# A hybrid attention and mLSTM layer on one core: the token transposes take over the scaling by the inverse roots

## The chip, the cores and the metric

The kernel runs on one core of one Trainium2 chip. The metric is the device time of one execution in microseconds (us), lower being better. The core has five engines that run side by side: TensorE (PE, with its weight loads shown apart as PEld), VectorE (DVE), ScalarE (ACT), GpSimd (POOL) and SyncE (SP), which issues most of the transfers. They synchronise through semaphores.

## The reference

The layer takes 1024 tokens of 1024 features. Only the first lines matter for this change:

```python
def rms_norm(x, w):
    xf = x.astype(jnp.float32)
    y = xf * lax.rsqrt(jnp.mean(xf * xf, axis=-1, keepdims=True) + RMS_EPS)
    return (y * w.astype(jnp.float32)).astype(x.dtype)

h = rms_norm(x, norm_w)
proj = jnp.einsum('btd,de->bte', h, w_in) + b_in
```

`proj` is 8720 columns wide. It is split into the inputs of a sliding-window attention and of an mLSTM. Their gated outputs go through two branch projections, a merge, an output projection with a residual, and a last RMS norm. Everything is fp32.

## The kernel before

**Tiling.** Tokens lie in `xs` as eight tiles of 128 tokens by 1024 features, tokens on partitions (`xs[:, t, :]`). The projection needs features on partitions, so TensorE turns every 128x128 block: `turn(t, k)` (L983 to L988) turns feature block `k` of token tile `t` into PSUM. Once the four tiles of a half (`t % 4 == 3`) are turned, block `k` of that half is a 128x512 tile in PSUM. ScalarE reads it, scales it by the norm weight and writes its high part in fp32r (`high_parts`, L1447, the operation at L1450); VectorE writes the low part, the rest (`low_parts`, L2121, the operation at L2125). The weights are split in the same way: `w_hi`, `w_lo`. A dense product is three fp32r products: high by high, low by high, high by low (`dense`, L957, the product at L973).

**The norm.** For tile `t`, ScalarE takes the sum of squares (`squares_of(t)`, L1441) once the tile has landed, VectorE makes a mean and adds epsilon (`variance(t)`, L2110), ScalarE takes the square root (`root(t)`, L1445), VectorE takes the reciprocal (L2114) and multiplies the whole 128x1024 tile in place (`normalised(t)`, L2119), and then TensorE may turn it (`turn_tile(t, ...)`, L993). Each queue is an order written out by hand.

**The order at the start.** TensorE: 24 transposes of the identity (L981), `turn_tile` 0 and 1, a transpose of the parameter rows (L1001) that ScalarE copies out (L1466), tile 2, the one block left out of tiles 0 to 2 (its bank held the parameters), tile 3, and then the first dense half tile (24 products, L1021), with `gate_tile(b, lo, hi)` (L1008, the product at L1015) beside the turns of the second half: four gate products, 12 turns of tiles 4 and 5, six gate products, 12 turns of tiles 6 and 7, six gate products, then the two blocks that found no free bank (8 turns), then the second dense half tile (L1035). From there on TensorE works through weight tiles that the other engines prepare: 32 pairs of tiles by a scheme of seven products (L1066), and the branch and output projections.

ScalarE: squares and roots of tiles 0 to 3 in turn (L1461), the copy of the parameters, `w_hi[0]` (L1469), `high_parts(0)`, squares and roots of tiles 4 to 7, `high_parts(1)`. VectorE: `variance` and `normalised` of tiles 0 to 3, `low_parts(0)`, the same of tiles 4 to 7, `low_parts(1)`. GpSimd waits for `w_hi[0]`, makes `w_lo[0]` in two halves (L828), and splits the gates' weights (L806, L808). SP issues the transfers: four tiles of x, the first weight tile, four more tiles of x (L582), the gates' weights as two transfers of 32-byte pieces (L584, L585), two gate biases, the sinks, and further weight tiles.

`ev` is an 8 KB buffer of two halves; the squares write their elementwise result, which nobody reads, to its first half.

Of the kernel before, what the change touches and what calls it, by code (L numbers as in the profile page):

```python
# [8 lines left out]
ALU = mybir.AluOpType  # L9
ACT = mybir.ActivationFunctionType  # L10
# [3 lines left out]
P = 128  # L14
# [3 lines left out]
NB = T // P  # L18
# [7 lines left out]
KB = 1024  # L26
# [94 lines left out]
def build(nc, x, norm_w, w_in, b_in, sinks, conv_w, conv_b, mnorm_w, wba, wbm, w_out, fnorm_w, out):  # L121
    ctx = ExitStack()
    with ctx:
        def sem(name):
            return ctx.enter_context(nc.semaphore(name))
# [5 lines left out]
        EV_AT = W_AT + 34 * KB  # L131
# [3 lines left out]
        def at(name, offset, shape, dt=F32):  # L135
            return nc.alloc_sbuf_tensor_at(name, shape, dt, offset=offset)

        def sb(name, shape, dt=F32):

            size = 4 if dt in (F32, F32R) else 2 if dt == BF16 else 1  # L140
            for n in shape[1:]:
                size *= n
            offset = kept[0]
            kept[0] += (size + 31) // 32 * 32
            return at(name, offset, shape, dt)
# [47 lines left out]
        w_raw = [at(f"w_raw{s}", W_AT + 4 * KB * s, [P, KT, P]) for s in range(2)]  # L193
        w_hi = [at(f"w_hi{s}", W_AT + o * KB, [P, KT, P], F32R) for s, o in enumerate((16, 8, 24))]
# [8 lines left out]
        squares = at("squares", W_AT + 20 * KB, [P, BANK])  # L203

        ev = at("ev", EV_AT, [P, 2, T])


        xs = at("xs", M_AT, [P, NB, T])
# [49 lines left out]
        ident = sb("ident", [P, P])  # L258
# [12 lines left out]
        rstd = sb("rstd", [P, 2 * NB])  # L271
# [18 lines left out]
        ps = ctx.enter_context(nc.psum_tensor("ps", [P, 8, BANK], F32))  # L290
# [32 lines left out]
        x_in = [sem(f"x_in{t}") for t in range(NB)]  # L323
        gate_slot_clear = sem("gate_slot_clear")
        w_in_sem = [sem(f"w_landed{s}") for s in range(2)]
# [3 lines left out]
        consts_made = sem("consts_made")  # L329
# [5 lines left out]
        x_norm = sem("x_norm")  # L335
# [106 lines left out]
        first_w_hi = sem("first_w_hi")  # L442
# [127 lines left out]
        x_rows = x.rearrange("(t p) d -> p t d", p=P)  # L570
# [5 lines left out]
        def _(sp):  # L576
# [1 line left out]
                sp.dma_start(xs[:, t, :], x_rows[:, t, :]).then_inc(x_in[t], 16)  # L578
            sp.dma_start(w_raw[0][:], w_cols[:, :, K0:K0 + P]).then_inc(w_in_sem[0], 16)

            for t in range(4, NB):
                sp.dma_start(xs[:, t, :], x_rows[:, t, :]).then_inc(x_in[t], 16)  # L582
            sp.wait_ge(gate_slot_clear, 1)
            sp.dma_start(w_raw[GATES][:, :, 0:8], w_cols[:, :, MI0:MF0]).then_inc(w_in_sem[GATES], 16)  # L584
            sp.dma_start(w_raw[GATES][:, :, 32:40], w_cols[:, :, MF0:MO0]).then_inc(w_in_sem[GATES], 16)  # L585
            sp.dma_start(gate_bias[0:8, :], b_in[MI0:MF0].rearrange("(h a) -> h a", a=1)).then_inc(vectors_in, 16)
            sp.dma_start(gate_bias[32:40, :], b_in[MF0:MO0].rearrange("(h a) -> h a", a=1)).then_inc(vectors_in, 16)
            sp.dma_start(sink_raw[:, :], sinks.partition_broadcast(P)).then_inc(vectors_in, 16)
# [107 lines left out]
            def weights(t0, tiles):  # L696

                cols = [c if isinstance(c, int) else sp.snap(c) for _, _, c in tiles]
                need = [n if isinstance(n, int) else sp.snap(n) for n in (t0 + j - 1 for j, _, _ in tiles)]
                for (j, src, _), c, n in zip(tiles, cols, need):  # L700
                    sp.wait_ge(w_split, n)
                    sp.sem_inc(passed, 1)

                    s = slot(BA + j)
                    sp.dma_start(w_raw[s][:], src[:, :, ds(c, P)]).then_inc(w_in_sem[s], 16)
# [248 lines left out]
        def _(pe):  # L954
# [27 lines left out]

            def turn(t, k):  # L983
                banks = BANKS[t // 4]
                mm = nc.tensor.transpose(ps[:, banks[k], (t % 4) * P:(t % 4 + 1) * P],
                                         xs[:, t, k * P:(k + 1) * P], ident[:])
                if t % 4 == 3:
                    mm.then_inc(x_turned, 1)  # L988

# [3 lines left out]
            def turn_tile(t, features):  # L993
                pe.wait_ge(x_norm, t + 1)
                for k in [k for k in range(features) if t >= 3 or k != table]:
                    turn(t, k)
# [7 lines left out]
            for t in range(3):  # L1004
                turn(t, table)
# [24 lines left out]
            for k in range(FRESH, KT):  # L1030
                pe.wait_ge(hT_lo_ready, KT + BANKS[1].index(BANKS[1][k]) + 1)
                for t in range(4, NB):
                    turn(t, k)
# [400 lines left out]
        def _(act):  # L1434
            A = nc.scalar.activation


            def squares_of(t):
                act.wait_ge(x_in[t], 16)
                act.drain()  # L1440
                A(ev[:, 0, :], xs[:, t, :], ACT.Square, accum_out=sumsq[:, t:t + 1]).then_inc(x_sumsq, 1)  # L1441

            def root(t):
                act.wait_ge(x_var, t + 1)
                A(rstd[:, t:t + 1], rstd[:, t:t + 1], ACT.Sqrt).then_inc(x_root, 1)  # L1445

            def high_parts(half):  # L1447
                for k in range(KT):
                    act.wait_ge(x_turned, KT * half + k + 1)
                    A(H[half][k // KH][0][:, k % KH, :], ps[:, BANKS[half][k], :], ACT.Copy,  # L1450
                      scale=par[:, R_NORM + k:R_NORM + k + 1]).then_inc(hT_hi_ready, 1)
# [3 lines left out]
            for row, src in ((R_NORM, norm_w), (R_Q, b_in[0:MI0]), (R_O, b_in[MO0:GM0 + D]), (R_MNORM, mnorm_w),  # L1455
# [2 lines left out]
                act.dma_start(param_rows[row:row + rows, :], src.rearrange("(r n) -> r n", n=P)).then_inc(params_in, 16)  # L1458
            act.dma_start(param_rows[R_CONVW:R_CONVW + 32, :],
                          conv_w.rearrange("j (r n) -> (j r) n", n=P)).then_inc(params_in, 16)  # L1460
            for t in range(3):  # L1461
                squares_of(t)
                root(t)
            squares_of(3)
            act.wait_ge(params_T, 1)
            A(par[:], ps[:, X[3], 0:ROWS], ACT.Copy).then_inc(params_ready, 1)  # L1466
            root(3)
            act.wait_ge(w_in_sem[0], 16)
            A(w_hi[0][:], w_raw[0][:], ACT.Copy).then_inc(first_w_hi, 1)  # L1469
            high_parts(0)  # L1470
            squares_of(4)
            squares_of(5)
# [631 lines left out]
        def _(dve):  # L2104
            V = nc.vector


            def variance(t):
                dve.wait_ge(x_sumsq, t + 1)
                V.tensor_scalar(rstd[:, t:t + 1], sumsq[:, t:t + 1], 1.0 / D, EPS, ALU.mult, ALU.add).then_inc(x_var, 1)  # L2110

            def inverse_root(t):
                dve.wait_ge(x_root, t + 1)
                return V.reciprocal(rstd[:, t:t + 1], rstd[:, t:t + 1])  # L2114

            def normalised(t):
                inverse_root(t)
                dve.drain()
                V.tensor_scalar(xs[:, t, :], xs[:, t, :], rstd[:, t:t + 1], None, ALU.mult).then_inc(x_norm, 1)  # L2119

            def low_parts(half):  # L2121
                for k in range(KT):
                    hi, lo = H[half][k // KH]
                    dve.wait_ge(hT_hi_ready, KT * half + k + 1)
                    V.scalar_tensor_tensor(lo[:, k % KH, :], ps[:, BANKS[half][k], :], par[:, R_NORM + k:R_NORM + k + 1],  # L2125
                                           hi[:, k % KH, :].bitcast(F32), ALU.mult, ALU.subtract).then_inc(hT_lo_ready, 1)

            for t in range(4):
                variance(t)
                normalised(t)  # L2130
            low_parts(0)
            variance(4)
            for t in range(4, NB):
                if t < NB - 1:
                    variance(t + 1)
                normalised(t)
# [664 lines left out]
```

## Time and profile before

| what | us |
|---|---|
| median of 3 runs (1077.52 to 1077.68) | 1077.52 |
| the profiled execution, its own time | 1077.55 |
| its span, first to last instruction | 1075.8 |
| TensorE busy | 1063.5 (99%) |
| VectorE busy | 725.9 (67%) |
| GpSimd busy | 649.7 (60%) |
| ScalarE busy | 516.9 (48%) |

The span is 1.75 us shorter than the time of the same execution. "Busy" counts an engine's instructions from start to end. TensorE's are pipelined, so what each costs in a stream is the distance between starts and not its duration. In a row of a timeline that covers several instructions of one kind, the second number runs from the first one's start to the last one's end; without the last one's own duration it is the distance from first to last start.

### The profile page before, as it was taken

The page shows a single profiled execution, that of the slowest core. Times are in us where ns is not written, and L with a number is a line of the kernel's source. Part 1 is how long each engine was busy: PE and PEld are TensorE (multiplying, and loading weights), DVE is VectorE, ACT ScalarE, POOL GpSimd, SP SyncE. Part 2 cuts the span into 40 slices and gives each one's busy share as a digit, 9 for nine tenths or more (in the row PEclk, how much of TensorE's full clock was granted, in tenths as well). Part 3 has the DMA queues.
Part 4 walks back from the last instruction along what each step waited for, and adds up shares of the span by engine and source line. Part 5 has one row for each costly group of instructions (what it writes and reads, how often), then busy time and mean ns, then how long its engine had stood idle before and what let it go on. Part 6 is the DMA issues. An engine that isn't in the chain of part 4 may idle for free.

```text
span 1075.8 us, 18631 instructions
## 1 busy us (share of the span) xinstructions
PE 1063.5 (99%) x6391; PEld 862.7 (80%) x6391; DVE 725.9 (67%) x1144; ACT 516.9 (48%) x1252; POOL 649.7 (60%) x437
## 2 busy tenths in 40 slices
PE   7999999999999999999999999999999999999997
PEld 6887887877877888878888888788788888888886
DVE  5964785776866967566756685669578332558897
ACT  7544755746647643555345444545464311132543
POOL 3577555556555568568955796679654354547441
PEclk9999999999999999999999999999999999999999
DMA  6235132132151231214211431143219434744324
GB/s 220 70 93 89 41 118 80 41 121 76 45 158 40 80 118 40 50 41 147 79 41 50 127 99 39 39 127 88 60 37 363 148 97 151 250 147 164 149 92 143
DMA packets 113851, 111.83 MB, mean 104 GB/s; under 512 B 7340, under 2 KB 96744, under 8 KB 112760
## 3 DMA queue, kind: packets, MB, share of 16 engines
q1 hardware_dynamic: 102648, 77.08, 24.2%
q10 hardware_dynamic: 11136, 33.88, 9.7%
q8 instruction: 39, 0.64, 0.2%
q14 instruction: 28, 0.23, 0.1%
HBM read 84.63 MB, written 26.31 MB: 103 GB/s over the span
## 4 chain that ended last, share of the span: by engine, by line
PE 97%; ACT 1%; DVE 1%; DMA 0%; DVEq 0%; issue 0%; ACTq 0%
PE ps L1066 64%; PE ps L1344 16%; PE ps L973 4%; PE ps L1178 3%; PE ps L1159 2%; PE ps L1233 2%; PE ps L1305 1%; PE ps L1287 1%; PE ps L1302 1%; ACT ev L1441 1%; PE ps L1299 1%; PE ps L1315 1%; PE ps L1253 1%; PE ps L1292 1%; PE ps L1015 1%; ACT h_hi L1450 0%
## 5 line engine op out<-in xcount | busy, mean ns | idle before, releaser
L823 POOL TENSOR_TENSOR ring_lo<-w,ring_hi 128x512 fp32r<-128x512 f32 x128 | 183.1, 1452 | 90.3 <-ACT ring_hi L1483 90.3
L823 POOL TENSOR_TENSOR ring_lo<-t,ring_hi 128x512 fp32r<-128x512 f32 x96 | 132.9, 1389 | 140.1 <-ACT ring_hi L1483 140.1
L1066 PE MATMUL ps<-s_hi,ring_hi 128*128 128x512 f32 x512 | 203.7, 398 | 0.0
L1066 PE MATMUL ps<-s_lo,ring_hi 128*128 128x512 f32 x512 | 200.2, 391 | 0.0
L1066 PE MATMUL ps<-s_hi,ring_lo 128*128 128x512 f32 x512 | 200.1, 391 | 0.0
L1066 PE MATMUL ps<-h_hi,ring_hi 128*128 128x512 f32 x384 | 151.6, 395 | 0.0
L1066 PE MATMUL ps<-h_lo,ring_hi 128*128 128x512 f32 x384 | 150.3, 392 | 0.0
L1066 PE MATMUL ps<-h_hi,ring_lo 128*128 128x512 f32 x384 | 149.9, 390 | 0.0
L1483 ACT ACTIVATE ring_hi<-w 128x512 fp32r<-128x512 f32 x128 | 77.0, 623 | 83.6 <-PE ps L1066 73.5
L1066 PEld LDWEIGHTS ps<-s_hi,ring_hi 128*128 128x128 f32 x512 | 96.2, 188 | 20.9 <-issue 2.5
L1066 PEld LDWEIGHTS ps<-s_hi,ring_lo 128*128 128x128 f32 x512 | 96.2, 188 | 20.0
L1066 PEld LDWEIGHTS ps<-s_lo,ring_hi 128*128 128x128 f32 x512 | 96.3, 188 | 18.4
L818 POOL TENSOR_TENSOR t<-w,t 128x512 f32<-128x512 f32 x64 | 96.8, 1512 | 9.0 <-issue 4.6
L1483 ACT ACTIVATE ring_hi<-t 128x512 fp32r<-128x512 f32 x96 | 59.9, 625 | 73.1 <-PE ps L1066 66.1
L806 POOL TENSOR_TENSOR w_hi<-w_raw,zero_col 128x1024 fp32r<-128x1024 f32 (+1 forms) x18 | 38.3, 2128 | 89.3 <-PE ps L1344 55.7
L1066 PEld LDWEIGHTS ps<-h_hi,ring_hi 128*128 128x128 f32 x384 | 72.3, 188 | 14.8 <-POOL ring_lo L823 0.7
L1066 PEld LDWEIGHTS ps<-h_hi,ring_lo 128*128 128x128 f32 x384 | 72.1, 188 | 14.8
L1066 PEld LDWEIGHTS ps<-h_lo,ring_hi 128*128 128x128 f32 x384 | 72.2, 188 | 13.9
L1344 PE MATMUL ps<-u_a,w_hi 128*128 128x512 f32 x256 | 78.9, 389 | 0.0
L1700 ACT ACTIVATE probs<-probs,neg_max 128x128 f32<-128x128 f32 x128 | 49.7, 390 | 41.3 <-DVE sink_in L2312 41.3
L1914 ACT ACTIVATE ev<-ev 128x1024 f32<-128x1024 f32 x16 | 17.0, 1062 | 107.6 <-DVE merged L2624 48.7
L1344 PE MATMUL ps<-u_m,w_hi 128*128 128x512 f32 x192 | 59.7, 392 | 0.0
(325 smaller groups left out, 2259.9 us busy)
## 6 DMA issues: line engine op xcount, KB each, us to landing
w<-in_w_in SPq DMA_DIRECT2D x128, 256.0 KB, 3.1
xs<-in_x SPq DMA_DIRECT2D x8, 512.0 KB, 7.5
ga_scratch<-ev ACTq DMA_DIRECT2D x4, 1024.0 KB, 4.2
u_scratch<-silu_z ACTq DMA_DIRECT2D x8, 512.0 KB, 3.2
c_rows<-c_scratch ACTq DMA_DIRECT2D x8, 512.0 KB, 6.1
gm_scratch<-ev ACTq DMA_DIRECT2D x4, 1024.0 KB, 5.0
w_raw<-in_w_branch_attn SPq DMA_DIRECT2D x8, 512.0 KB, 4.1
u_a_f<-u_scratch SPq DMA_DIRECT2D x4, 1024.0 KB, 8.4
```

The lines of the kernel that those rows point to most:

```text
L806: nc.gpsimd.tensor_tensor(hi, src, zero_col[:].to_broadcast(list(src.shape)), ALU.add)
L818: return nc.gpsimd.tensor_tensor(flat(dst), flat(a), flat(b), op)
L823: return nc.gpsimd.tensor_tensor(flat(lo[:]), flat(raw_or_sum[:]), flat(hi[:]).bitcast(F32), ALU.subtract)
L973: mm = nc.tensor.matmul(ps[:, 2 * s + b, :], w[:, k, :], h[:, k % KH, :], start=(r == 0), stop=(r == KT * TERMS - 1))
L1066: mm = nc.tensor.matmul(ps[:, bank, columns], w[:, k, :], h[:, k, columns], start=(m == 0), stop=(m == PRODUCT - 1))
L1159: mm = nc.tensor.matmul(ps[64 * half:64 * half + 64, SCORES[r], column:column + keys], q_T[rows, j, queries], k_now[rows, first:first + keys],
L1178: mm = nc.tensor.matmul(pv_ps(slice(64 * r, 64 * r + 64), half), v_m, pT[rows, 2 * r:2 * r + 2, queries], start=start, stop=stop)
L1233: mm = nc.tensor.transpose(ps[:, TURNED, h * P:(h + 1) * P], probs[n % 2][:, h, :], ident[:])
L1344: mm = nc.tensor.matmul(ps[:, 2 * s + b, :], w[:, k, :], part(k)[(0, 1, 0)[term]][:, token_half(b)], start=starts, stop=stops)
L1483: return A(ring_slot[0][:], raw_or_sum[:], ACT.Copy)
L1700: A(pr[:, h, :], pr[:, h, :], ACT.Exp, scale=HD ** -0.5, bias=neg_max[:, h:h + 1], accum_out=row_sum[:, h:h + 1])
L1914: A(ev[:, j, :], ev[:, j, :], ACT.Tanh, scale=0.5).then_inc(gate_tanh, 1)
```

## The change

The tokens are no longer multiplied in place. For each tile VectorE writes `scales[:, t, :]`, the 128x128 identity with row p times the inverse root of token p, into the second half of the `ev` buffer. `turn(t, k)` becomes an ordinary fp32 product of the raw block with `scales[:, t, :]`. On ScalarE the squares of tile t + 1 come ahead of the root of tile t for tiles 0 to 3, and `w_hi[0]` moves from ScalarE to VectorE, after the scaling of tile 3. On VectorE the variance of tile t + 1 comes ahead of the scaling of tile t, and VectorE waits for the identity. On SP the gates' weights are issued ahead of the last two tiles of x.

```diff
+        scales = at("scales", EV_AT + 4 * KB, [P, NB, P])
...
-            for t in range(4, NB):
+            for t in range(4, 6):
                 sp.dma_start(xs[:, t, :], x_rows[:, t, :]).then_inc(x_in[t], 16)
             sp.wait_ge(gate_slot_clear, 1)
             sp.dma_start(w_raw[GATES][:, :, 0:8], w_cols[:, :, MI0:MF0]).then_inc(w_in_sem[GATES], 16)
             sp.dma_start(w_raw[GATES][:, :, 32:40], w_cols[:, :, MF0:MO0]).then_inc(w_in_sem[GATES], 16)
+            for t in range(6, NB):
+                sp.dma_start(xs[:, t, :], x_rows[:, t, :]).then_inc(x_in[t], 16)
...
             def turn(t, k):
                 banks = BANKS[t // 4]
-                mm = nc.tensor.transpose(ps[:, banks[k], (t % 4) * P:(t % 4 + 1) * P],
-                                         xs[:, t, k * P:(k + 1) * P], ident[:])
+                mm = nc.tensor.matmul(ps[:, banks[k], (t % 4) * P:(t % 4 + 1) * P],
+                                      xs[:, t, k * P:(k + 1) * P], scales[:, t, :], start=True, stop=True)
...
-            for t in range(3):
+            squares_of(0)
+            for t in range(1, 4):
                 squares_of(t)
-                root(t)
-            squares_of(3)
+                root(t - 1)
             act.wait_ge(params_T, 1)
             A(par[:], ps[:, X[3], 0:ROWS], ACT.Copy).then_inc(params_ready, 1)
             root(3)
-            act.wait_ge(w_in_sem[0], 16)
-            A(w_hi[0][:], w_raw[0][:], ACT.Copy).then_inc(first_w_hi, 1)
             high_parts(0)
...
             def normalised(t):
                 inverse_root(t)
                 dve.drain()
-                V.tensor_scalar(xs[:, t, :], xs[:, t, :], rstd[:, t:t + 1], None, ALU.mult).then_inc(x_norm, 1)
+                V.tensor_scalar(scales[:, t, :], ident[:], rstd[:, t:t + 1], None, ALU.mult).then_inc(x_norm, 1)
...
+            dve.wait_ge(consts_made, 1)
+            variance(0)
             for t in range(4):
-                variance(t)
+                if t < 3:
+                    variance(t + 1)
                 normalised(t)
+            dve.wait_ge(w_in_sem[0], 16)
+            V.tensor_scalar(w_hi[0][:], w_raw[0][:], 1.0, None, ALU.mult).then_inc(first_w_hi, 1)
             low_parts(0)
```

## Rows read from the trace of the kernel before

**Rows 1.** The page: busy time of the engines over the span.
```profile
PE 1063.5 (99%) x6391; PEld 862.7 (80%) x6391; DVE 725.9 (67%) x1144; ACT 516.9 (48%) x1252; POOL 649.7 (60%) x437
```
**Rows 2.** The waits of TensorE, whole span: us in total, times, longest us.
```profile
PE ps L985 <- DVE xs L2119: 2.9, 5, 0.9
PE ps L981 <- POOL ident L795: 2.2, 1, 2.2
PE ps L973 <- DVE h_lo L2125: 0.9, 1, 0.9
```
**Rows 3.** The timeline, first half of the tokens: start us, us, instruction.
```profile
4.95 1.06 ACT L1441 ACTIVATE ev<-xs 128x1024 f32<-128x1024 f32 x1 [2.63 <-DMA xs<-in_x]
...
6.13 0.15 DVE L2110 TENSOR_SCALAR rstd<-sumsq 128x1 f32<-128x1 f32 x1 [6.13 <-ACT ev L1441]
...
6.79 0.75 DVE L2119 TENSOR_SCALAR xs<-xs,rstd 128x1024 f32<-128x1024 f32 x1
...
7.60 0.98 PE L985 MATMUL ps<-ident,xs 128*128 128x128 f32 x7 [0.92 <-DVE xs L2119]
...
11.39 1.04 ACT L1469 ACTIVATE w_hi<-w_raw 128x1024 fp32r<-128x1024 f32 x1
...
12.56 1.10 PE L985 MATMUL ps<-ident,xs 128*128 128x128 f32 x8 [0.34 <-DVE xs L2119]
12.93 4.74 ACT L1450 ACTIVATE h_hi<-ps,par 128x512 fp32r<-128x512 f32 x8 [0.50 <-PE ps L985]
...
14.55 0.47 PE L973 MATMUL ps<-h_hi,w_hi 128*128 128x512 f32 x1 [0.89 <-DVE h_lo L2125]
```
**Rows 4.** The same timeline, second half of the tokens.
```profile
18.98 1.06 ACT L1441 ACTIVATE ev<-xs 128x1024 f32<-128x1024 f32 x1
...
20.04 0.19 ACT L1445 ACTIVATE rstd<-rstd 128x1 f32<-128x1 f32 x1
...
20.50 0.75 DVE L2119 TENSOR_SCALAR xs<-xs,rstd 128x1024 f32<-128x1024 f32 x1
...
20.79 0.39 PE L1015 MATMUL ps<-h_lo,w_hi 128*128 128x512 f32 x1
...
21.31 0.88 PE L985 MATMUL ps<-ident,xs 128*128 128x128 f32 x6
...
24.74 1.47 PE L985 MATMUL ps<-ident,xs 128*128 128x128 f32 x12
...
28.54 0.50 PE L973 MATMUL ps<-s_hi,w_hi 128*128 128x512 f32 x1
```
**Rows 5.** The chain that ended last, a stretch of dense products: start us, us, what.
```profile
37.91 22.21 PE ps L973 x98
```
**Rows 6.** TensorE by line, an fp32 product: records, busy us, mean ns.
```profile
L1305 PE MATMUL ps<-v,dmat 128*128 128x129 f32 x128 | 20.0, 278 | 0.0
```
**Rows 7.** The timeline at 434 us: two fp32 products, their loads and their passes.
```profile
434.50 0.58 PEld L1305 LDWEIGHTS ps<-v,dmat 128*128 128x128 f32 x4
434.66 0.61 PE L1305 MATMUL ps<-v,dmat 128*128 128x129 f32 x4
```
**Rows 8.** Transfers of x: tiles 1 and 2 (L578), then the landings of tiles 4 to 7 (L582).
```profile
L578 SPq DMA_DIRECT2D xs<-in_x x2: 422/427/432, 1.3 to 1.7; - x2
DMA to landing us min/median/max: 4.9/5.4/5.9
...
DMA to landing us min/median/max: 8.2/8.7/10.0
```
**Rows 9.** The timeline of GpSimd, the low part of the first weight tile.
```profile
12.51 2.51 POOL L828 TENSOR_TENSOR w_lo<-w_raw,w_hi 128x512 fp32r<-128x512 f32 x2 [7.99 <-ACT w_hi L1469]
```
**Rows 10.** The timeline of SP's queue: the gates' second transfer, then a bias.
```profile
7.40 5.09 SPq L585 DMA_DIRECT2D w_raw<-in_w_in  x1
12.53 3.20 SPq L586 DMA_DIRECT2D gate_bias<-in_b_in  x1
```
**Rows 11.** All engines, 21 to 28.5 us; the last columns are PEclk, DMA share, GB/s.
```profile
21.00:28.50 7.50, 6.92 (x45) 5.62 (x44) 5.18 (x13) 4.80 (x12) 3.47 (x2) 1.00 0.23 67
```

## The prediction

> **What bounds the kernel now.** I read the page first: TensorE is busy for 99% of the span [rows 1]. Then its waits: it waits three times for another engine, 2.2 us for the identity, 2.9 us in five pieces for normalised tiles before a turn, 0.9 us for the first low part [rows 2], and all of it lies before 23 us. From there to the end no wait of TensorE is listed. So whatever delays the second dense half tile (28.54 us, [rows 4]) delays the end by as much, since every later stage starts from what TensorE has done. And the change can win at most what TensorE waits there. The question is how early the dense products start, and what TensorE itself must do before them.
>
> In the timeline a tile's chain is squares, mean, root, reciprocal, scaling, turn. The first tile's squares start at 4.95 when it lands, its turns at 7.60; the fourth tile's turns at 12.56, the first high part at 12.93, the first dense product at 14.55 [rows 3]. Between turns TensorE idles: seven take 0.98 us, and each next tile comes 1.65 us later.
>
> **What a turn costs.** This carries the forecast. Twelve transposes take 1.47 us from first start to last end [rows 4], one lasts 0.27, so starts lie (1.47 - 0.27) / 11 = 0.109 us apart; in short runs 0.118: (0.98 - 0.27) / 6 [rows 3]. The new turn is an fp32 product without the transpose flag. The kernel has such ones. The twelve transposes of tiles 6 and 7 have 12 records [rows 4]. L1305 is an fp32 product that the source issues twice for each of 8 chunks of 4 head pairs, 64 times, and it has 128 records [rows 6]: an fp32 product is two passes with two weight loads. Two of them together take 0.61 us for four passes, the last 0.275 long, so passes start (0.61 - 0.275) / 3 = 0.112 us apart [rows 7], with 129 columns. A new turn therefore holds TensorE for p = 2 x 0.112 = 0.224 us, against 0.11 to 0.12. Bounds: two passes at the transposes' pitch, 0.218; two at the pitch of the loads, (0.58 - 0.19) / 3 = 0.13 [rows 7], 0.26. I take 0.224, since shape, type and form are those of L1305.
>
> The trace knows a transposed block at 0.109 us and a pass of a product at 0.112, a ratio of 2.05 for the whole turn. The Trainium skill (TensorE: Matmul & The Clock Gate, Terms) says that the transpose mode makes fp32 four times faster; by that a turn would cost 4 x 0.109 = 0.436 us and the sum below would be 15.4 us. The trace does not agree for this shape.
>
> **Part 1, the first tiles.** Squares 1 can start when x tile 1 lands, 1.3 + 4.9 = 6.2 [rows 8], instead of 6.60. Its root of tile 0 now stands behind it: start 6.25 + 1.06 = 7.31 (a root follows squares by 1.06, 18.98 to 20.04 [rows 4]), end 7.50, scaling 0.27 later (20.23 to 20.50 [rows 4]) at 7.77. The scaling shrinks from 128x1024 to 128x128: 0.15 us is the length of a 128x1 operation, 0.75 that of the 1024-wide one [rows 3], so about 0.15 + 0.60 / 8 = 0.23. Turns of tile 0 start at 8.05, which is 0.45 later than now. Squares 2 and 3 follow at about 7.7 and 9.05; scaling 1 and 2 are ready at 9.5 and 10.9, and tile 3, with the parameters' copy between, at about 12.6.
>
> TensorE does not get there in time. Ahead of the first turn of tile 3 stand 7 + 7 + 7 + 3 = 24 turns and the transpose of the parameters (0.12): 8.05 + 24 x 0.224 + 0.12 = 13.55, against 12.56. From 8.05 on TensorE has no idle time, so earlier roots and shorter scalings buy nothing. The first high part needs one whole turn more, 0.11 longer than now. Delay of the first high part, and with it of the whole dense half tile: 13.55 - 12.56 + 0.11 = **1.10 us**. The other turns of tile 3 at 0.224 each stay ahead of the high parts, which go at 4.74 / 8 = 0.59 [rows 3].
>
> **Part 2, `w_hi[0]` on VectorE.** It leaves ScalarE, where it took 1.04 us ahead of the high parts in what was waiting time anyway [rows 3]: worth nothing. VectorE does it after scaling 3, from about 12.65, in 0.75 us by the row of the same shape [rows 3]; if its fp32r output halved the pace it would be 1.5. GpSimd then makes the first half of `w_lo[0]` in 1.25 us [rows 9], ready at 14.7 (or 15.4). The third dense product wants it at 14.55 + 1.10 + 0.45 = 16.1. Hidden, with 0.7 us left in the worse case. Were the cover gone, the cost would be that lateness. VectorE's low parts wait for the first high part, which starts at 14.03, so `w_hi[0]`, done at 13.4, does not hold them (at 14.15 it would not either, since the high part takes 0.59).
>
> **Part 3, tiles 4 to 7.** Take the times of before and add 1.10 at the end. The last of the first four gate products starts at 20.79; a 512-wide product holds TensorE 22.21 / 98 = 0.227 us [rows 5], so TensorE is free at 21.02, while the turns of tile 4 start at 21.31 [rows 4]. Scaling 4 now ends 0.53 earlier (20.73), and TensorE goes straight on: this gains 0.29, and the idle time before tile 5, some 0.5 us, is filled too. Then TensorE has 12 turns, 6 gate products, 12 turns, 6 gate products, 8 turns: 32 x 0.224 + 12 x 0.227 = 9.89, from 21.02 to 30.91. Squares go on at 1.33 us a tile, so scaling 5 (22.05) and 7 (24.3) are ready before their turns (22.4 and 26.4). The low parts that the last turns and the dense products wait for follow the first turn of tile 7 and are ready about 1.3 us before 30.9. Before, the first dense product of the second half streamed from 28.54 + 0.11 = 28.65 (it lasts 0.50 instead of 0.39, its load included). Delay: 30.91 - 28.65 = **2.26 us**.
>
> **Part 4, SP.** The two transfers of the gates' weights go past tiles 6 and 7. TensorE has no wait for their split even now [rows 2], and its first gate product comes 1.10 later: landing sooner gains nothing. Tiles 6 and 7 move behind an issue that took 5.09 us and another that took 3.20 [rows 10]; the cost of that is a rival. The wait for the identity on VectorE costs nothing, since TensorE has used it at 2.2 us [rows 2].
>
> **Sum.** 1.10 + 2.26 = +3.4 us; in general 57 p - 9.4. At 0.218 it is 3.0, at 0.26 it is 5.4. The profiled execution took 1077.55, within 0.03 of the median 1077.52. Forecast: 1080.9 us. The granted clock was 1.00 in this stretch [rows 11], so the prices are those of the full clock.
>
> **Rivals.**
> - *The new turn costs one pass* (the other side, not slower). Place: the 64 turns. Below p = 9.4 / 57 = 0.165 the change wins, and then other engines set the pace: tile 3 is scaled at about 11.6, its turns start 0.85 earlier, and in the second half some 0.5 of waiting goes. 1077.5 - 1.35 = 1076.2, which a measurement could hardly tell from no change. Against it: 128 records for 64 products. 4%.
> - *Only part of the delay gets through.* If the passes overlap better than rows 7 show, or the turns between gate products hide in their loads, p falls to 0.2 and the sum to 2.0: 1079.5. For it: short runs are read from few records. Against: TensorE shows no idle time among the short runs that such hiding could use. 9%.
> - *A turn costs four transposes.* Each of its two passes streams at half the pace of a transposed block, p = 4 x 0.109 = 0.436, and TensorE pays it 64 times: 57 x 0.436 - 9.4 = 15.4 us, 1092.9. Against: passes would start 0.218 apart and rows 7 have 0.112. 4%. (This is the skill's rule above.)
> - *Tile 7 lands late.* If SP is held for 5.09 us until 12.5 and for 3.2 more, and tile 7 needs the 10.0 us of the slowest x tile [rows 8], it lands at 25.7. Its squares, root and scaling take 2.1, and its turns are due at 27.5: 0.3 late, 1081.2; twice such holds would give 1084. For it: the small pieces really did hold the queue. Against: nearly 3 us of slack, and fewer bytes stand ahead. 8%.
> - *Forecast*: two passes at 0.218 to 0.26, 75%.
>
> **How the numbers follow.** About 0.2%, 2.15 us, is what a measurement of this kernel can tell from no change. The forecast case, the late tile and the four transposes are slower by more (87%, less a little for the forecast's lower edge: 86%). The middle case and the one pass lie within it (13%); I move 2 of these to a gain that I have not seen (the one pass with more waiting filled) and 1 from the slower cases: 3%, 11%, 86%. The range goes from 1079.2, which takes in most of the middle case, to 1083.0 (p = 0.26); outside are the one pass, the four transposes, and the edge of the late tile.
>
> **What would show it.** L985 should have 128 records instead of 64, with starts 0.11 us apart, and TensorE almost no wait between 8.05 and the dense products except for the first low part (0.9 or less). Turns of tile 0 near 8.05, first high part near 14.0, first dense product near 15.65, second dense half tile near 31.9. VectorE's scalings near 0.23 and `w_hi[0]` near 0.75. From there on both traces should run in parallel, 3.4 us apart. A first high part before 12.9, or 64 records, would make it wrong; so would a wait of TensorE after 32 us in the trace of before that I took for none.

## The result and the profile after

The changed kernel takes 1081.06 us (median of 7 runs, 1080.79 to 1081.37) against 1077.52 (1077.28 to 1077.68) beside it. The ratio is 1.0033, with a 95% interval of 1.0021 to 1.0045: it is 3.5 us slower. Its profiled execution took 1081.37, the slowest of the seven, with a span of 1079.7.

The page first, the line of engine busy times, against [rows 1]:

```profile
PE 1070.3 (99%) x6455; PEld 870.6 (81%) x6455; DVE 725.5 (67%) x1145; ACT 515.3 (48%) x1251; POOL 644.3 (60%) x437
```

TensorE has 64 records more and 6.8 us more busy time. The waits of TensorE over the whole span, against [rows 2] (us in total, times, longest):

```profile
PE ps L984 <- POOL ident L798: 2.2, 1, 2.2
PE ps L988 <- DVE scales L2120: 0.9, 1, 0.9
```

Of the five waits for a normalised tile one is left, the first; the wait for the first low part is gone too. Nearly all of that waiting has been filled, and the kernel is slower all the same. The operations by line within the first 34 us say with what (records, busy us, mean ns):

```profile
L988 PE MATMUL ps<-scales,xs 128*128 128x128 f32 x128 | 15.4, 277 | 0.9 <-DVE scales L2120 0.9
...
L2120 DVE TENSOR_SCALAR scales<-ident,rstd 128x128 f32<-128x128 f32 x8 | 2.3, 286 | 0.6
```

The 64 turns have 128 records, as the L1305 products had [rows 6]. The timeline, against [rows 3, 4] (start us, us, instruction):

```profile
6.06 1.06 ACT L1444 ACTIVATE ev<-xs 128x1024 f32<-128x1024 f32 x1
...
7.87 1.06 ACT L1444 ACTIVATE ev<-xs 128x1024 f32<-128x1024 f32 x1 [0.57 <-DMA xs<-in_x]
...
7.92 3.64 PE L988 MATMUL ps<-scales,xs 128*128 128x128 f32 x28 [0.92 <-DVE scales L2120]
...
9.39 0.29 DVE L2120 TENSOR_SCALAR scales<-ident,rstd 128x128 f32<-128x128 f32 x1
9.73 1.64 PEld L988 LDWEIGHTS ps<-scales,xs 128*128 128x128 f32 x14 [0.18 <-DVE scales L2120]
...
11.51 4.19 PE L988 MATMUL ps<-scales,xs 128*128 128x128 f32 x36
...
12.54 0.69 DVE L2136 TENSOR_SCALAR w_hi<-w_raw 128x1024 fp32r<-128x1024 f32 x1
13.31 2.50 POOL L831 TENSOR_TENSOR w_lo<-w_raw,w_hi 128x512 fp32r<-128x512 f32 x2 [8.81 <-DVE w_hi L2136]
...
14.17 4.74 ACT L1453 ACTIVATE h_hi<-ps,par 128x512 fp32r<-128x512 f32 x8 [2.10 <-PE ps L988]
...
15.78 0.47 PE L976 MATMUL ps<-h_hi,w_hi 128*128 128x512 f32 x1
...
22.27 2.84 PE L988 MATMUL ps<-scales,xs 128*128 128x128 f32 x24
...
26.34 2.84 PE L988 MATMUL ps<-scales,xs 128*128 128x128 f32 x24
...
32.10 0.48 PE L976 MATMUL ps<-s_hi,w_hi 128*128 128x512 f32 x1
```

The first dense product is 1.23 us later than before (15.78 against 14.55), the second dense half tile 3.56 later (32.10 against 28.54). A long run of 24 passes takes 2.84 us, the last 0.27 long: (2.84 - 0.27) / 23 = 0.112 us from start to start. After that both traces run in parallel. Two pieces of the chain that ended last, from the middle and from the start of the output projection (the kernel before has the same pieces at 798.20 and 993.37):

```profile
801.72 15.00 PE ps L1069 x66
...
997.25 70.78 PE ps L1069 x312
```

The distance is 3.52 us at 800 us and 3.88 at 997. The medians are 3.54 apart, so the last third of a microsecond probably belongs to this execution, the slowest of the seven. The profiled execution of one other kernel, turns_twice, shows the same step, from 17.09 to 17.43; what makes it stays open.

### The profile page after: what moved, and what is told of

It is laid out like the page before. It is cut to its first block, busy times and chain, and to the rows that moved or that the text cites. A ratio compares the mean times of both kernels' runs of the same rounds, so it can differ in the third digit from the quotient of the medians.

```text
span 1079.7 us, 18760 instructions
## 1 busy us (share of the span) xinstructions
PE 1070.3 (99%) x6455; PEld 870.6 (81%) x6455; DVE 725.5 (67%) x1145; ACT 515.3 (48%) x1251; POOL 644.3 (60%) x437
## 4 chain that ended last, share of the span: by engine, by line
PE 98%; DVE 1%; DMA 0%; ACT 0%; DVEq 0%; issue 0%; SPq 0%; ACTq 0%
PE ps L1069 63%; PE ps L1347 16%; PE ps L976 4%; PE ps L1181 3%; PE ps L1162 2%; PE ps L1236 2%; PE ps L1308 1%; PE ps L988 1%; PE ps L1290 1%; PE ps L1305 1%; PE ps L1302 1%; PE ps L1018 1%; PE ps L1318 1%; PE ps L1256 1%; PE ps L1295 1%; DMA xs<-in_x 0%
## 5 line engine op out<-in xcount | busy, mean ns | idle before, releaser
L826 POOL TENSOR_TENSOR ring_lo<-w,ring_hi 128x512 fp32r<-128x512 f32 x128 | 186.5, 1478 | 96.0 <-ACT ring_hi L1484 96.0
L809 POOL TENSOR_TENSOR w_hi<-w_raw,zero_col 128x1024 fp32r<-128x1024 f32 (+1 forms) x18 | 34.0, 1890 | 92.5 <-PE ps L1347 57.5
```

The source lines that it names most:

```text
L809: nc.gpsimd.tensor_tensor(hi, src, zero_col[:].to_broadcast(list(src.shape)), ALU.add)
L826: return nc.gpsimd.tensor_tensor(flat(lo[:]), flat(raw_or_sum[:]), flat(hi[:]).bitcast(F32), ALU.subtract)
```

## The experiments

The table gives the medians and three marks: the first high part, the first dense product, and the first of the second dense half tile. The marks are of one execution each, the profiled one. Its own time is up to 0.45 us from the median, in roots_first_16 0.67.

| kernel | median us | high part | dense | second dense |
|---|---|---|---|---|
| before | 1077.52 | 12.93 | 14.55 | 28.54 |
| after | 1081.06 | 14.17 | 15.78 | 32.10 |
| turns_only | 1080.30 | 12.90 | 14.52 | 30.82 |
| roots_first | 1080.29 | 13.25 | 14.87 | 31.19 |
| transposes_unscaled | 1076.71 | 12.49 | 14.11 | 27.63 |
| turns_twice | 1094.75 | 19.36 | 22.20 | 45.63 |
| second_half_old | 1079.54 | 13.83 | 15.45 | 29.44 |
| old_whi_and_dma | 1080.76 | 13.71 | 15.33 | 31.65 |
| tile3_only | 1077.90 | 12.56 | 14.18 | 28.16 |
| tile3_gates | 1077.40 | 12.43 | 14.04 | 27.56 |
| roots_first_16 | 1081.43 | 14.92 | 16.54 | 32.85 |
| before_16 | 1077.59 | 13.35 | 14.97 | 28.96 |

### turns_only: the turns alone, all orders as before

```diff
-nc.tensor.transpose(..., xs[:, t, k * P:(k + 1) * P], ident[:])
+nc.tensor.matmul(..., xs[:, t, k * P:(k + 1) * P], scales[:, t, :], start=True, stop=True)
...
-V.tensor_scalar(xs[:, t, :], xs[:, t, :], rstd[:, t:t + 1], None, ALU.mult)
+V.tensor_scalar(scales[:, t, :], ident[:], rstd[:, t:t + 1], None, ALU.mult)
```

VectorE also waits for the identity first, as in the full change.

> The kernel before with the scaled identity and the fp32 products alone: ScalarE takes the roots in the old order, w_hi[0] stays on ScalarE, SP issues in the old order. Theory A (the passes of the turns carry the loss, and the new order of squares and roots adds to it, since the first turn starts 0.9 us later behind the squares of tile 1 while TensorE has work from there on): first turn near 7.1, first high part near 13.2, second dense half tile about 2.5 us later than before, 1080.0. Theory B (the passes alone, the order is neutral): 1081.0, as the full change. Theory C (the loss comes from order, w_hi or transfers): at most 1078.

Measured: 1080.30 (1079.85 to 1080.67), ratio 1.0026 [1.0016, 1.0036]. That is theory A: with roots in the old order the first high part is not late at all (12.90 against 12.93), and the loss is made in the second half: 30.82 - 14.52 = 16.30 us between the two marks instead of 28.54 - 14.55 = 13.99, so 2.31. The profiled execution (1079.85) is the fastest of the nine, 0.45 below their median, so in most runs the first half is probably not quite free.

### roots_first: the change with the old order of squares and roots

```diff
-squares_of(0)
-for t in range(1, 4):
-    squares_of(t)
-    root(t - 1)
+for t in range(3):
+    squares_of(t)
+    root(t)
+squares_of(3)
...
-variance(0)
 for t in range(4):
-    if t < 3:
-        variance(t + 1)
+    variance(t)
     normalised(t)
```

> The changed kernel with the old order of squares and roots for tiles 0 to 3 on ScalarE and of variances on VectorE; all else as changed. Theory A: first turn near 7.0 instead of 7.92, about 0.9 us gained to the end, 1080.1. Theory B (order neutral, as the turns wait for the last tile's scaling anyway): 1081.0. Theory D (squares first does help, as it was written to): 1081.5 or more.

Measured: 1080.29 (1080.01 to 1080.72), ratio 1.0026 [1.0016, 1.0036]. Theory A again: 0.8 us better than the full change, the first dense product 0.91 earlier. The new order is a loss in itself. It was to take roots off the path of the squares, but once each tile costs TensorE 1.6 us, the first scaling decides and not the last. Of the 0.91 us, 0.56 stand ahead of the first turn (7.36 against 7.92). The other 0.35 lie within the turns of the first two tiles, 28 passes in 3.29 us against 3.64, since the full change waits there for the second scaling. The gain could have been larger. The timeline of this kernel shows the first scaling done at 6.60 + 0.28 = 6.88, but the turns start at 7.36, right behind the transposes of the identity, the last of which starts at 7.19:

```profile
2.23 5.29 PE L984 MATMUL ps<-ident 128*128 128x128 f32 x24 [2.23 <-POOL ident L798]
...
6.60 0.28 DVE L2120 TENSOR_SCALAR scales<-ident,rstd 128x128 f32<-128x128 f32 x1
...
7.36 3.29 PE L988 MATMUL ps<-scales,xs 128*128 128x128 f32 x28
```

### transposes_unscaled: one pass a turn, the scaling of the tokens left out

```diff
-nc.tensor.matmul(..., xs[:, t, k * P:(k + 1) * P], scales[:, t, :], start=True, stop=True)
+nc.tensor.transpose(..., xs[:, t, k * P:(k + 1) * P], ident[:])
```

> The changed kernel with the turns as transposes of the raw tokens; the scaling by the inverse roots is left out, all waits and VectorE's scalings stay. Theory A: with one pass a turn the small scalings come through: tile 3's turns near 11.9 instead of 12.56, tiles 4 and 5 without a wait, 1076.4. Theory C (something else in the change costs): 1077.5 or more.

Measured: 1076.71 (1076.32 to 1077.65), ratio 0.9994 [0.9985, 1.0003]. The second dense half tile starts 0.91 earlier than before, and the kernel is 4.35 us faster than the full change. So the second pass costs 4.35 us, and everything else in the change together gains about 0.8. The direction is theory A's; it had asked for 0.3 more, and the interval just takes in no change.

### turns_twice: every turn issued twice

```diff
+for again in range(2):
     mm = nc.tensor.matmul(ps[...], xs[:, t, k * P:(k + 1) * P], scales[:, t, :], start=True, stop=True)
```

> The changed kernel with every turn issued twice into the same place: 64 fp32 products more, two passes each. Theory A: TensorE pays 57 of them at 0.224 us (seven of tile 3 hide behind the high parts): +12.8 us, 1093.9. If the cost of a turn were mostly hidden, +6 or less; if each pass cost more than the starts show, +15 or more.

Measured: 1094.75 (1094.42 to 1095.02), 13.7 us above the change. In the second half 32 turns more cost (45.63 - 22.20) - (32.10 - 15.78) = 7.11 us, 0.222 us each. The miss is in the first half, where the expectation let seven turns of tile 3 hide behind the high parts. They do not, because all eight stand ahead of the dense products in TensorE's own order:

```profile
14.24 8.21 PE L989 MATMUL ps<-scales,xs 128*128 128x128 f32 x72
...
19.36 4.74 ACT L1454 ACTIVATE h_hi<-ps,par 128x512 fp32r<-128x512 f32 x8 [4.55 <-PE ps L989]
```

The high parts start at 19.36, but the 72 passes run to 22.45. The first dense product enters TensorE right behind the last of them, at 22.20, which is 2.84 behind the first high part instead of 1.61.

### second_half_old: tiles 4 to 7 as before

```diff
-    mm = nc.tensor.matmul(..., xs[:, t, k * P:(k + 1) * P], scales[:, t, :], start=True, stop=True)
+    if t < 4:
+        mm = nc.tensor.matmul(..., xs[:, t, k * P:(k + 1) * P], scales[:, t, :], start=True, stop=True)
+    else:
+        mm = nc.tensor.transpose(..., xs[:, t, k * P:(k + 1) * P], ident[:])
```

VectorE's scaling is split in the same way, by `t < 4`.

> The changed kernel with tiles 4 to 7 scaled in place and transposed as before; tiles 0 to 3 as changed. Theory A (two separate shares, 1.24 us by the first half's 25 turns and 2.3 by the second's 32): the second share goes, 1078.8, with some 0.5 us of waiting before tiles 4 and 5 back. If the first half were free: 1077.5; if it carried most: 1080 or more.

Measured: 1079.54 (1079.21 to 1081.88), ratio 1.0022 [1.0013, 1.0031]. Up to the second dense half tile the sum holds: 29.44 - 15.45 = 13.99 us between the marks, as in the kernel before, so the second half's share is 16.32 - 13.99 = 2.33 us. But the median is 0.7 above the expectation, and the trace has a wait of TensorE that neither the kernel before nor the change shows; it ends at 634.7 us. TensorE is 0.90 us behind the kernel before up to there and 1.63 behind from there on. This step has the size of what is missing, though only this one execution shows it; tile3_only has the same wait, and below it is followed to its source.

### old_whi_and_dma: `w_hi[0]` on ScalarE, the gates' weights last

```diff
-dve.wait_ge(w_in_sem[0], 16)
-V.tensor_scalar(w_hi[0][:], w_raw[0][:], 1.0, None, ALU.mult).then_inc(first_w_hi, 1)
+act.wait_ge(w_in_sem[0], 16)
+A(w_hi[0][:], w_raw[0][:], ACT.Copy).then_inc(first_w_hi, 1)
...
-for t in range(4, 6):
+for t in range(4, NB):
     sp.dma_start(xs[:, t, :], x_rows[:, t, :]).then_inc(x_in[t], 16)
...
-for t in range(6, NB):
-    sp.dma_start(xs[:, t, :], x_rows[:, t, :]).then_inc(x_in[t], 16)
```

> The changed kernel with w_hi[0] back on ScalarE and the gates' weights issued behind tiles 6 and 7 of x. Theory A: both are hidden, 1081.1 within 0.2. Rival: w_hi on VectorE frees ScalarE for the high parts and is worth some of 1 us, then 1081.5 to 1082.

Measured: 1080.76 (1080.73 to 1081.28), ratio 1.0031 [1.0019, 1.0042]. The rival falls. Theory A's figure is missed by 0.1; between the first dense product and the second half tile both kernels need 16.32 us. The 0.3 us between the medians stays open. In the two profiled executions all of the distance lies before the first dense product: the first turn is 0.21 earlier (7.71 against 7.92), and the turns of the first two tiles are 0.25 shorter (3.39 against 3.64), where the full change waits for the second scaling and so for x tile 2. The runs of either kernel spread over nearly 0.6 us.

### tile3_only and tile3_gates: can part of the idea pay?

```diff
+    if t == 3:
+        mm = nc.tensor.matmul(..., xs[:, t, k * P:(k + 1) * P], scales[:, t, :], start=True, stop=True)
+    else:
         mm = nc.tensor.transpose(..., xs[:, t, k * P:(k + 1) * P], ident[:])
```

VectorE's scaling is split in the same way, by `t == 3`; VectorE waits for the identity first.

> The kernel before with only tile 3 turned by products with its scaled identity. Theory A: its scaling is 0.46 us shorter while TensorE and everybody behind it waits for it, its products hide behind the high parts' 0.59 a block except for half of the first: 1077.5 - 0.35 = 1077.2. Rival: the extra passes show in full, +0.9: 1078.4.

Measured: 1077.90, ratio 0.9999 [0.9990, 1.0008]. The start goes as theory A says: the second dense half tile is 0.38 earlier. The eleven runs fall into two groups, five from 1077.11 to 1077.40 and six from 1077.90 to 1078.05. The profiled one (1078.05) is of the second group, and among TensorE's waits it has one more:

```profile
PE ps L1071 <- POOL ring_lo L824: 0.5, 1, 0.5
```

It ends at 633.5 us. TensorE is 0.36 ahead of the kernel before at 546 us and 0.37 behind at 637. These 0.73 us are about the distance of the two groups; no run of the faster group was profiled, so that the groups differ by this wait is likely and not shown. GpSimd delivers the low part of a weight tile too late there. Here is the operation that makes it, in tile3_only and in the kernel before:

```profile
632.14 1.27 POOL L824 TENSOR_TENSOR ring_lo<-w,ring_hi 128x512 fp32r<-128x512 f32 x1
...
630.78 2.28 POOL L823 TENSOR_TENSOR ring_lo<-w,ring_hi 128x512 fp32r<-128x512 f32 x1
```

In the kernel before the low part is ready at 633.06, here at 633.41, while TensorE comes 0.36 earlier. GpSimd starts this operation 1.36 us later than in the kernel before, and the traces show from where. At 601 us it is still 0.37 ahead, like TensorE. Then it waits for a weight tile, in tile3_only and in the kernel before:

```profile
606.02 2.79 POOL L819 TENSOR_TENSOR t<-w,w 128x512 f32<-128x512 f32 x1 [4.05 <-DMA w<-in_w_in]
...
604.19 1.29 POOL L818 TENSOR_TENSOR t<-w,w 128x512 f32<-128x512 f32 x1 [1.87 <-DMA w<-in_w_in]
```

The transfer that it waits for was issued at 597.16 and took 8.7 us to land; in the kernel before it was issued at 597.51 and took 6.5. By 615 us that leaves GpSimd 0.37 behind the kernel before. Of the next three operations (`ring_lo<-w`) one takes 2.29 us instead of 1.30, and from there on it is 1.35 behind.

It is the transfer and not TensorE's lead that goes with the wait. In the profiled executions it took 8.5 to 8.7 us in tile3_only, tile3_gates and second_half_old, the three kernels whose traces show the wait, and 6.5 to 7.0 us in the nine others. second_half_old comes to this place 0.90 us later than the kernel before and waits; transposes_unscaled comes 0.91 earlier and does not. Why the transfer took two microseconds more was not tested. In every trace SP and ScalarE issue six transfers here within some 3 us, this one among them.

In tile3_gates the gate products are laid in pieces of 6, 2, 2 and 6:

```diff
-gate_tile(0, 0, 4)
+gate_tile(0, 0, 6)
 turn_tile(4, FRESH)
+gate_tile(0, 6, 8)
 turn_tile(5, FRESH)
-gate_tile(0, 4, 10)
+gate_tile(0, 8, 10)
```

> As tile3_only, and the 16 gate products laid around the turns of tiles 4 to 7 in pieces of 6, 2, 2 and 6 instead of 4, 6 and 6, so that TensorE works while it now waits for the scalings of tiles 4 and 5. Theory A: that wait moves to tile 7's scaling, which ends at 24.8 whatever TensorE does, so only about 0.25 of the 0.8 us comes through: 1077.0. Rival: all of it, 1076.4; or nothing, as tile3_only.

Measured: 1077.40, ratio 0.9996 [0.9987, 1.0005]. Again two groups: five runs from 1076.46 to 1076.91 and six from 1077.40 to 1078.21. Between the marks it needs 13.52 us where tile3_only needs 13.98, so 0.46 comes through, between theory A and the rival. At 27.56 the second half tile is 0.98 ahead of the kernel before, and the same wait, here at 633 us, takes 0.7 back in the profiled run. No version here beats the kernel before beyond the noise of the medians. But the five faster runs of tile3_gates lie below every run of the kernel before (1077.12 or more): the gain at the start is there, and whether it reaches the end seems to hang on that transfer.

### roots_first_16 and before_16: fewer transposes of the identity

```diff
-for n in range(3 * KT):
+for n in range(2 * KT):
```

> roots_first with 16 transposes of the identity at the start instead of 24. In roots_first the first scaled identity is ready at 6.88, but the 24 transposes end at 7.52 and the first turn queues behind them. Theory E (only the queue holds it): the 16 end near 5.7, the first turn starts near 6.95, 0.5 us gained, 1079.8. Theory F (the starts of the early passes lie 0.213 us apart until some 6 to 7 us whatever runs, and fewer transposes in front leave more of that to the turns): nothing gained or a loss, 1080.3 or more, and passes of tile 0 at 0.2 us.

> The kernel before with 16 transposes of the identity at the start instead of 24. Its first turns start at 7.60, behind their own scaling. Theory E: no change, 1077.4 within 0.1. Theory F: the turns of tiles 0 and 1 run at 0.213 us apart, hidden at first in TensorE's waits of 0.9 and 0.7 us, so 1077.4 to 1078.

Measured: roots_first_16 1081.43, in two groups: four runs from 1079.82 to 1080.08, which is theory E's time, and five from 1081.43 to 1082.30, which is theory F and worse. The profiled one, 1082.10, is of the second group, so what the four faster ones did is not shown:

```profile
2.22 3.67 PE L984 MATMUL ps<-ident 128*128 128x128 f32 x16 [2.22 <-POOL ident L798]
6.84 5.47 PE L988 MATMUL ps<-scales,xs 128*128 128x128 f32 x28 [0.94 <-DVE scales L2120]
```

The 28 passes of the first two tiles take 5.47 us, 0.19 apart in the mean, against 3.29 in roots_first: 19 of the 27 distances are 0.213 or more, the last ones 0.11. The column of the granted clock reads 1.00 through all of that (rows of the windows; after the busy times stand granted clock, DMA share, GB/s):

```profile
8.00:10.00 2.00, 2.00 (x12) 2.00 (x11) 0.87 (x5) 1.70 (x4) 0.00 (x0) 1.00 1.19 324
```

before_16 has 1077.59 (1077.37 to 1078.18), ratio 1.0002 [0.9993, 1.0011]. Its profiled execution (1078.04) has the first dense product 0.42 late, and here the rows of the windows do show the clock:

```profile
8.00:10.00 2.00, 1.33 (x11) 1.10 (x10) 1.24 (x4) 1.62 (x5) 0.00 (x0) 0.91 1.15 329
10.00:12.00 2.00, 1.89 (x10) 1.49 (x9) 1.41 (x4) 1.94 (x5) 0.00 (x0) 0.50 1.02 403
12.00:14.00 2.00, 2.00 (x14) 1.83 (x12) 0.41 (x1) 0.98 (x3) 1.59 (x2) 0.73 1.04 414
```

TensorE idled for 1.61 us ahead of its first turns and for 0.67 ahead of those of the next tile. Within a tile the turns up to 9.66 start 0.109 us apart; then the granted clock fell to 0.50, the lower level of 1.2 GHz, and up to 13 us they start 0.213 apart. That is theory F in this execution; the median, 1077.59, cannot be told from the kernel before. With 16 transposes roots_first_16 spreads over 2.5 us where roots_first spreads over 0.7: there the start becomes a matter of luck.

## Why the prediction was right

The forecast was 1080.9, the measured median 1081.06; the sum was +3.4 us, the change costs +3.5.

- **What a turn costs.** Right. 128 records; p = 0.224 forecast, 2 x 0.1117 = 0.223 in the long runs of the change and 0.222 in turns_twice. The kernel's own L1305 was the right row to price from. The Trainium skill's factor of four for fp32 (TensorE: Matmul & The Clock Gate, Terms) does not hold here: this case's trace gives 0.223 against 0.109, a factor of 2.05 for 128 columns. The rivals of one pass and of four transposes fall with it, and so does the one in which only part of the delay gets through.
- **Part 1, +1.10 forecast.** Measured +1.24 at the first high part (14.17 against 12.93). First turn 7.92 instead of 8.05, so the rest is 0.27 more than forecast. The step that was off is "from 8.05 on TensorE has no idle time": x tile 2 landed at 7.8, squares 2 waited 0.57 us for it, the root of tile 1 stood behind them by the new order, and so did scaling 1, done at 9.68 instead of 9.5. The load of the second tile's turns waited 0.18, and by the distances of starts TensorE lost 0.25 us there, nearly all of the 0.27. A scaling takes 0.29, not 0.23. That the new order itself costs was said (the first turn 0.45 later), but not that it is nearly a quarter of the loss, as roots_first shows: 0.8 of 3.5 us.
- **The high part's one extra pass, +0.11.** Right in size, and less safe than it was put. The first dense product still stands 1.61 us behind the first high part, as before (1.62), so the first low part still sets it. The view no longer lists that wait, 0.9 us before [rows 2], because tile 3's own turns now fill it: their last pass starts at 15.43 and ends at 15.70, and the first dense product starts at 15.78, where the distance of starts alone would let it in at 15.54. So some 0.2 us were to spare for the seven turns behind the first one. With a turn that costs over 0.03 us more, the delay would have grown by all 32 turns of the half and not by 25. turns_twice ran into that.
- **Part 2.** Hidden, as forecast. `w_hi[0]` runs from 12.54 for 0.69 us and GpSimd starts at 13.31; old_whi_and_dma takes it back and changes nothing that can be told from noise.
- **Part 3, +2.26 forecast.** Measured 2.33, by the distance of the marks (16.32 against 13.99), and the same from turns_only and second_half_old.
- **Part 4.** Nothing gained and nothing lost. SP's queue held the second of the gates' transfers for 2.99 us and tile 6 for 3.91, tile 7 was issued at 13.2 and landed 5.0 us later, at 18.2; its squares start at 22.87. That rival had nearly five microseconds of slack:

```profile
6.23 2.99 SPq L586 DMA_DIRECT2D w_raw<-in_w_in  x1
9.26 4.39 SPq L588 DMA_DIRECT2D xs<-in_x  x2
```

- **From there on in parallel.** Right: 3.54 us at 100 us, 3.52 at 800. But that "every later stage starts from what TensorE has done" was nearer to failing than the prediction saw. The prediction read the waits of TensorE's products and found none. The weight loads (PEld) have waits of their own, and the kernel before shows one at the place where three experiments lost 0.7 us:

```profile
633.11 0.19 PEld L1066 LDWEIGHTS ps<-h_hi,ring_hi 128*128 128x128 f32 x1 [0.23 <-POOL ring_lo L823]
```

There GpSimd had nothing to spare already. One transfer that took two microseconds longer made it a wait of TensorE, whether TensorE came earlier (tile3_only) or later (second_half_old). The profiled execution of the change had the transfer in 6.9 us and was spared; its seven runs spread over 0.6 us, so none shows such a step clearly. That part was luck that the forecast had no term for.

## What to carry to other kernels

Before a transpose is merged with a scaling by giving up the transpose flag, count the records of an fp32 product that the kernel already has: two passes a block, paid by TensorE, for a VectorE operation that was partly hidden, is a bad trade where TensorE is the bound, even when it removes nearly every wait in the stage. Reordering a chain so that its last link comes earlier delays its first one; that pays only while the consumer waits for the last. And an engine at 99% with no listed waits need not have slack in front of it: read the waits of its weight loads too, since the next 0.7 us may hang on a single transfer 30 us ahead.

## What the runs showed of the hardware

**The pace of the first transposes.** The 24 transposes of the identity have starts 0.213 us apart at first and 0.109 later, and the moment of the step differs from trace to trace. In eight of the ten profiled kernels with 24 of them it lies between 5.6 and 6.5 us; in roots_first and tile3_gates all 24 are 0.213 apart, and the turns behind them run at the faster pace. So they ended between 6.68 (before) and 7.60 us (tile3_gates), with 16 of them at 5.89. The granted clock in the rows reads 1.00 from 2 to 8 us (before, roots_first), so here the distance of starts told more than the column. In before_16 the column did show 0.50 after idle times of 1.61 and 0.67 us, and there the distances of starts agree with it.

**Small fp32 products.** An fp32 pass of 128 columns starts 0.112 us after the last, a transpose of the same block 0.109; the flag saves the second pass, and next to nothing else at this size.

**Two paces of one GpSimd operation.** GpSimd's two-input operation on 128x512 takes 1.27 or 2.28 us within a few microseconds. In the kernel before 302 of 376 take about 1.3 us and 33 take 2.28. During each of the 33 VectorE works for at least 80% of the time, but it also works beside most of the fast ones (65% in the mean), so it may depend on which operation stands there; no run tested it. A schedule that is written for one pace can miss by a microsecond in the other.

**One transfer, two landing times.** The same weight tile, issued together with five other transfers (at 597 us in the kernel before), took 6.5 to 7.0 us to land in nine profiled executions and 8.5 to 8.7 in three. The later landings are the ones that TensorE waits for at 633 us.
